# Self-attention of a hybrid decoder layer: value products per head with the values stationary in two f32r parts, and the output weights split inside the stage

## Chip, cores and metric

The kernel runs on one core of one Trainium2 chip. The time is device time in microseconds of one execution of the whole layer. Engines are called by the letters of the profile: PE (matmul), DVE (VectorE), ACT (ScalarE), POOL (GpSimd), SP (the engine that issues most DMAs).

## What is computed

One layer with three sub-layers over 1024 positions of width 1024, in f32. Only the first, the hybrid token mixer, is touched. Its part C is causal attention with 8 heads, query and key width 96, value width 64:

```
sc = einsum('bqhd,bkhd->bhqk', q_blk, k) * scale
mask = key_pos <= q_pos
p = softmax(where(mask, sc, -inf))
o = einsum('bhqk,bkhd->bqhd', p, v)
...
return concatenate([ret, sgu, mla], axis=-1) @ w_out
```

The 512 columns of `mla` are the last four of the eight 128-row slices over which the product with `w_out` (1024x1024) sums.

## The kernel before

The layer is a sequence of stages with a barrier between two of them: `project`, `prepare`, `attend`, `mix_out`, `cross_attend`, `experts`, `overflow`. Inside a stage each engine runs a list written out by hand and waits on counting semaphores. Two stages matter here.

**`attend`.** The work is cut into 48 units. For the first four query tiles (128 queries each, i = 0 to 3) a unit is a pair of heads, for i = 4 to 7 it is one head. The outer loop goes over i, the inner one over heads. For each unit PE makes the scores (queries stationary, up to 512 keys moving, f32, L704), DVE adds the causal mask to the diagonal 128 columns (L784) and takes the negated row maximum (L788, L790), ACT takes the exponential with the row sum (L748, L751), PE transposes the probabilities 128 columns at a time (L714), DVE copies the first and ACT the second transposed bank to SBUF (L797, L760), and PE multiplies (L725): the transposed probabilities are stationary, and 64 columns of values move, in f32. At the end of a query tile DVE divides by the row sums (L773, L774) and leaves `mix_mla` with the tokens in the partitions. Scores, transposes and outputs have two PSUM buffers each. In each round PE issues scores of unit u, values of unit u-2, transposes of unit u-1. Meanwhile SP loads `w_out` and fills DRAM buffers with zeros (L685 to L690).

**`mix_out`.** For each of 8 token tiles PE transposes eight 128x128 blocks of the mixer's output (L866), ACT rounds them to a high f32r part (L906), DVE makes the low part by subtraction (L924), and PE sums 8 slices x 2 halves x 3 products of high and low parts (L883 to L885). The weights are split in the same way, eight slices of 1024 columns, on ACT (L902) and DVE (L935), after the first tile's parts. DVE then waits for `x` and two broadcast gains (`loaded`) before it makes the parts of the second tile. SP loads the weights of the next stage after the last split.

In the functions below, `P` is 128, `MH` 8, `MV` 64, `NT` 8, `KD` 8, `S` and `D` 1024. `k.x` are tiles shared by the stages. In SBUF, `at(name, kb, shape)` places a tile at an offset in KB.

Of the kernel before, what the change touches and what calls it, by code (L numbers as in the profile page):

```python
# [15 lines left out]
P = 128  # L16
# [76 lines left out]
def over(ap, shape):  # L93
    return ap.broadcast_to(shape)
# [562 lines left out]
def attend(nc, k):  # L657
    at, A, cst = k.at, k.dram, k.cst
    prob = at("prob", 12, [P, 2, 2, 4 * P])
    probT = at("prob_T", 20, [P, 2, 2, 4 * P])  # L660
    nmx = at("neg_max", 28, [P, 2, 2])
    rsum = at("row_sum", 28.0625, [P, NT, MH])
    rinv = at("row_inv", 28.5, [P, NT, MH])
    zeros = at("zeros", 185, [P, ROW])
    ident = cst[:, C_ID:C_ID + P]
    units = [(i, h) for i in range(NT) for h in range(0, MH, 2 if i < 4 else 1)]

    scored = k.sem("scored")
    max_ready = k.sem("max_ready")
    exps = k.sem("exps")  # L670
    p_t = k.sem("p_t")
    pT_copied = k.sem("pT_copied")
    pT_copied_act = k.sem("pT_copied_act")
    pv_done = k.sem("pv_done")
    o_taken = k.sem("o_taken")
    dve_chain, zeroed = k.sem("chain3"), k.sem("zeroed")
    with nc.psum_tensor("s_ps", [P, 2, 2, 512], f32) as sps, \
# [4 lines left out]
        @block.sync  # L682
        def _(sp):
            for s in range(KD):
                sp.dma_start(k.w_out_raw[:, s, :], A["w_out"][s * P:(s + 1) * P, :]).then_inc(k.w_out_loaded, 16)  # L685

            sp.wait_ge(zeroed, 1)
            for t in range(SLOTS // P):
                sp.dma_start(k.xs_dram[t * P:(t + 1) * P, :], zeros[:]).then_inc(k.rows_zeroed, 16)
                sp.dma_start(k.z_dram[t * P:(t + 1) * P, :], zeros[:, 0:D]).then_inc(k.rows_zeroed, 16)  # L690

        def parts(u):

            i, h = units[u]
            return [(h, 0, i + 1), (h + 1, 0, i + 1)] if i < 4 else [(h, 0, 4), (h, 4, i + 1)]

        @block.tensor
        def _(pe):
            def scores(u):
                i = units[u][0]  # L700
                if u >= 2:
                    pe.wait_ge(exps, 2 * (u - 1))
                for j, (h, a, z) in enumerate(parts(u)):
                    last = pe.matmul(sps[:, u % 2, j, 0:(z - a) * P], k.qT[0:MQ, h, i * P:(i + 1) * P], k.kT[0:MQ, h, a * P:z * P],  # L704
                                     start=True, stop=True)
                last.then_inc(scored, 1)

            def turn(u):
                pe.wait_ge(exps, 2 * (u + 1))
                for j, (h, a, z) in enumerate(parts(u)):  # L710
                    if u:
                        pe.wait_ge(pT_copied if j == 0 else pT_copied_act, u)
                    for m in range(z - a):
                        last = pe.transpose(tps[:, j, m * P:(m + 1) * P], prob[:, u % 2, j, m * P:(m + 1) * P], ident)  # L714
                    last.then_inc(p_t, 1)

            def values(u):
                i, h0 = units[u]
                pe.wait_ge(pT_copied, u + 1)
                pe.wait_ge(pT_copied_act, u + 1)  # L720
                if h0 == 0 and i >= 2:
                    pe.wait_ge(o_taken, i - 1)
                for j, (h, a, z) in enumerate(parts(u)):
                    for m in range(a, z):
                        last = pe.matmul(ops[:, i % 2, h * MV:(h + 1) * MV], probT[:, u % 2, j, (m - a) * P:(m - a + 1) * P],  # L725
                                         k.v[:, m, h * MV:(h + 1) * MV], start=(m == 0), stop=(m == i))
                last.then_inc(pv_done, 1)

            n = len(units)
            for u in range(n + 2):  # L730
                if u < n:
                    scores(u)
                if 0 <= u - 2:
                    values(u - 2)
                if 0 <= u - 1 < n:
                    turn(u - 1)

        @block.scalar
        def _(act):
            for u in range(len(units) + 1):  # L740
                if u < len(units):
                    i, h = units[u]
                    act.wait_ge(max_ready, u + 1)
                    if u >= 2:
                        act.wait_ge(p_t, 2 * (u - 1))
                    if i < 4:
                        for j in range(2):
                            act.activation(prob[:, u % 2, j, 0:(i + 1) * P], sps[:, u % 2, j, 0:(i + 1) * P], ACT.Exp,  # L748
                                           bias=nmx[:, u % 2, j:j + 1], accum_out=rsum[:, i, h + j:h + j + 1]).then_inc(exps, 1)
                    else:  # L750
                        act.activation(prob[:, u % 2].rearrange("p j n -> p (j n)")[:, 0:(i + 1) * P],  # L751
                                       sps[:, u % 2].rearrange("p j n -> p (j n)")[:, 0:(i + 1) * P], ACT.Exp,
                                       bias=nmx[:, u % 2, 0:1], accum_out=rsum[:, i, h:h + 1]).then_inc(exps, 2)
                if u >= 1:
                    v = u - 1
                    _, a, z = parts(v)[1]
                    act.wait_ge(p_t, 2 * (v + 1))
                    if v >= 2:
                        act.wait_ge(pv_done, v - 1)
                    act.activation(probT[:, v % 2, 1, 0:(z - a) * P], tps[:, 1, 0:(z - a) * P], ACT.Copy).then_inc(pT_copied_act, 1)  # L760

        @block.vector
        def _(dve):
            chain = [0]

            def link(ins):
                chain[0] += 1
                ins.then_inc(dve_chain, 1)
                dve.wait_ge(dve_chain, chain[0])

            def take(i):
                dve.wait_ge(pv_done, units.index((i + 1, 0)) if i + 1 < NT else len(units))
                link(dve.reciprocal(rinv[:, i, :], rsum[:, i, :]))  # L773
                dve.tensor_tensor(k.mixB[:, i, :].rearrange("p (h d) -> p h d", d=MV),  # L774
                                  ops[:, i % 2, :].rearrange("p (h d) -> p h d", d=MV),
                                  over(rinv[:, i, :, None], [P, MH, MV]), ALU.mult).then_inc(o_taken, 1)

            for u in range(len(units) + 1):
                if u < len(units):
                    i, h = units[u]  # L780
                    dve.wait_ge(scored, u + 1)
                    s = sps[:, u % 2].rearrange("p j n -> p (j n)")
                    d = sps[:, u % 2, :, i * P:(i + 1) * P] if i < 4 else s[:, None, i * P:(i + 1) * P]
                    link(dve.tensor_tensor(d, d, over(cst[:, None, C_MASK:C_MASK + P], [P, d.shape[1], P]), ALU.add))  # L784
                    if u >= 2:
                        dve.wait_ge(exps, 2 * (u - 1))
                    if i < 4:
                        dve.tensor_reduce(nmx[:, u % 2, :], sps[:, u % 2, :, 0:(i + 1) * P], AX.X, ALU.max, negate=True).then_inc(max_ready, 1)  # L788
                    else:
                        dve.tensor_reduce(nmx[:, u % 2, 0:1], s[:, 0:(i + 1) * P], AX.X, ALU.max, negate=True).then_inc(max_ready, 1)  # L790
                if u >= 1:
                    v = u - 1
                    _, a, z = parts(v)[0]
                    dve.wait_ge(p_t, 2 * v + 1)
                    if v >= 2:
                        dve.wait_ge(pv_done, v - 1)
                    dve.tensor_copy(probT[:, v % 2, 0, 0:(z - a) * P], tps[:, 0, 0:(z - a) * P]).then_inc(pT_copied, 1)  # L797
                    if units[v][0] and v == units.index((units[v][0], 0)) + 1:
                        take(units[v][0] - 1)
            take(NT - 1)  # L800

        @block.gpsimd
        def _(pool):
            pool.memset(zeros[:], 0.0).then_inc(zeroed, 1)


# [5 lines left out]
def mix_out(nc, k):  # L812
# [3 lines left out]
    wraw = k.w_out_raw  # L816
    whi = at("wo_hi", 105, [P, KD, D], f32r)
    wlo = at("wo_lo", 137, [P, KD, D], f32r)
# [20 lines left out]
    with nc.psum_tensor("mixT_ps", [P, 2, 2, 512], f32) as tps, \  # L839
# [4 lines left out]
        def _(sp):  # L844
# [5 lines left out]
            sp.wait_ge(w_lo, KD)  # L850
# [5 lines left out]
            sp.wait_ge(mix_t, NT)  # L856
# [3 lines left out]
        def _(pe):  # L860
            def turn(t):
                if t >= 2:
                    pe.wait_ge(m_lo, t - 1)
                for j in range(KD):
                    src = k.mixA if j < 4 else k.mixB
# [5 lines left out]
            for t in range(NT):  # L871
# [1153 lines left out]
```

## Time and profile before

| | |
|---|---|
| median of 3 runs | 1056.36 us (1054.65 to 1058.7) |
| profiled execution | 1056.7 us, its span 1054.4 us |
| PE busy | 976.8 us, 93% |
| DVE busy | 607.2 us, 58% |
| ACT busy | 353.9 us, 34% |
| POOL busy | 191.0 us, 18% |
| mean granted PE clock | 0.962 |

A busy PE is not a PE at its peak: matmuls overlap in the pipeline and the profile models their ends. How long a stream of them takes is read from the starts. An f32 matmul appears as two records, an f32r matmul and a transpose as one. In the trace both types are written f32, except where DVE or ACT writes fp32r.

### The profile page before, as it was taken

To read this page: it belongs to the slowest core of one execution; us is meant where nothing else is said; L and a number is where in the kernel's file an instruction comes from. 1 tells how busy PE (TensorE), PEld (TensorE's weight loads), DVE (VectorE), ACT (ScalarE), POOL (GpSimd) and SP (SyncE) were. 2 spreads that over 40 slices of the span, in tenths; PEclk is the share of its full clock that TensorE was granted. 3 is DMA by queue.
4 is the path that set the end of the run, shared out by engine and by line. 5 is a ranking of instruction groups with operands and counts; after the bars stand their busy time and mean duration, and the time that the engine had idled before them with its cause. 6 is when DMAs were issued, how large, how long until landed. Compare 5 with 4: busy or idle time off the path is not lost. (4 is left out here: it accounts for less than half of the span.)

```text
span 1054.4 us, 15610 instructions
## 1 busy us (share of the span) xinstructions
PE 976.8 (93%) x5507; PEld 820.1 (78%) x5507; DVE 607.2 (58%) x1268; ACT 353.9 (34%) x736; POOL 191.0 (18%) x272
## 2 busy tenths in 40 slices
PE   7999999999899999899999999997289999999995
PEld 5898877767778887688885888886279898888984
DVE  6634341777566655455472455347526767676675
ACT  6112121343444333410013232331134445444442
POOL 0022100121000000012220000002414453434334
PEclk9999999999699999899999999998579999999998
DMA  9022010000798000370203200031748889899972
GB/s 334 13 77 80 1 61 1 1 1 1 305 413 328 1 1 2 120 277 3 80 1 123 80 1 1 1 133 69 300 153 261 296 269 316 280 319 314 318 286 89
DMA packets 63735, 150.46 MB, mean 143 GB/s; under 512 B 10304, under 2 KB 12608, under 8 KB 63680
## 3 DMA queue, kind: packets, MB, share of 16 engines
q1 hardware_dynamic: 54720, 132.77, 35.8%
q0 software_dynamic: 8960, 16.96, 4.3%
q8 instruction: 34, 0.56, 0.2%
q14 instruction: 21, 0.17, 0.1%
HBM read 109.46 MB, written 54.92 MB: 156 GB/s over the span
## 5 line engine op out<-in xcount | busy, mean ns | idle before, releaser
L1627 PEld LDWEIGHTS h_ps<-xgT,e_gate_up 128*128 128x128 f32 x1024 | 156.3, 192 | 4.2 <-issue 1.9
L1627 PE MATMUL h_ps<-xgT,e_gate_up 128*128 128x176 f32 x1024 | 157.8, 316 | 1.7 <-ACT xgT L1661 1.7
L245 PE MATMUL unit_ps<-whi,xhi 128*128 128x512 f32 (+1 forms) x256 | 98.3, 384 | 9.6 <-DVE wlo L276 9.6
L246 PE MATMUL unit_ps<-wlo,xhi 128*128 128x512 f32 (+1 forms) x256 | 97.8, 382 | 0.0
L247 PE MATMUL unit_ps<-whi,xlo 128*128 128x512 f32 (+1 forms) x256 | 97.7, 382 | 0.0
L725 PEld LDWEIGHTS o_ps<-mla_v,prob_T 128*128 128x128 f32 x576 | 72.6, 197 | 15.4 <-issue 10.5
L704 PE MATMUL s_ps<-mla_kT,mla_qT 96*128 96x512 f32 (+3 forms) x192 | 74.3, 515 | 3.4 <-PEq L1978 3.4
L725 PE MATMUL o_ps<-mla_v,prob_T 128*128 128x64 f32 x576 | 72.3, 276 | 2.8 <-ACT prob_T L760 2.5
L245 PEld LDWEIGHTS unit_ps<-whi,xhi 128*128 128x128 f32 x256 | 48.6, 190 | 18.1 <-DVE xlo L315 7.3
L247 PEld LDWEIGHTS unit_ps<-whi,xlo 128*128 128x128 f32 x256 | 48.5, 189 | 7.8
L246 PEld LDWEIGHTS unit_ps<-wlo,xhi 128*128 128x128 f32 x256 | 48.6, 190 | 7.5
L1692 ACT ACTIVATE ln_junk<-z,z_neg_mean 128x1024 f32<-128x1024 f32 (+1 forms) x32 | 36.8, 1149 | 52.1 <-DVE z_neg_mean L1751 51.6
L1746 DVE SCALAR_TENSOR_TENSOR z<-y_ps,slot_weight,x_rows 128x512 f32<-128x512 f32 (+1 forms) x64 | 45.7, 746 | 14.0 <-PE y_ps L1639 13.8
L751 ACT ACTIVATE prob<-s_ps,neg_max 128x640 f32<-128x640 f32 (+3 forms) x32 | 30.6, 955 | 67.7 <-issue 63.9
L883 PE MATMUL mix_acc<-wo_hi,mixT_hi 128*128 128x512 f32 x128 | 51.1, 399 | 2.2 <-DVE wo_lo L935 2.2
L1637 PE MATMUL y_ps<-e_dn_hi,h_hi 128*128 128x512 f32 (+1 forms) x128 | 52.0, 406 | 0.9 <-DVE z L1746 0.9
L704 PEld LDWEIGHTS s_ps<-mla_kT,mla_qT 96*128 96x128 f32 x192 | 35.2, 211 | 22.6 <-issue 20.9
L884 PE MATMUL mix_acc<-wo_lo,mixT_hi 128*128 128x512 f32 x128 | 50.5, 395 | 0.0
L885 PE MATMUL mix_acc<-wo_hi,mixT_lo 128*128 128x512 f32 x128 | 50.4, 394 | 0.0
L1639 PE MATMUL y_ps<-e_dn_hi,h_lo 128*128 128x512 f32 (+1 forms) x128 | 50.2, 393 | 0.0
L1638 PE MATMUL y_ps<-e_dn_lo,h_hi 128*128 128x512 f32 (+1 forms) x128 | 50.0, 391 | 0.0
L1714 DVE SCALAR_TENSOR_TENSOR ln_out<-ln_tmp,z_rstd,ln_b 128x1024 f32<-128x1024 f32 (+1 forms) x34 | 42.0, 1277 | 5.1 <-POOL z_rstd L1594 5.1
(280 smaller groups left out, 1930.9 us busy)
## 6 DMA issues: line engine op xcount, KB each, us to landing
e_gate_up<-w_gu SPq DMA_DIRECT2D x16, 2048.0 KB, 11.1
e_down_raw<-w_dn SPq DMA_DIRECT2D x16, 1024.0 KB, 5.4
slot_rows<-zeros SPq DMA_DIRECT2D x22, 522.0 KB, 14.8
slot_sums<-zeros SPq DMA_DIRECT2D x22, 512.0 KB, 15.2
x_rows<-slot_rows SPq DMA_DIRECT2D x16, 522.0 KB, 4.7
slot_sums<-z SPq DMA_DIRECT2D x16, 512.0 KB, 4.5
wraw<-w_in SPq DMA_DIRECT2D x24, 256.0 KB, 4.6
xraw<-xT SPq DMA_DIRECT2D x8, 512.0 KB, 6.8
```

The lines of the kernel that those rows point to most:

```text
L245: pe.matmul(o, hi, whi[:, s, 0:w], start=(s == 0), stop=False)
L246: pe.matmul(o, hi, wlo[:, s, 0:w], start=False, stop=False)
L247: last = pe.matmul(o, lo, whi[:, s, 0:w], start=False, stop=(s == KD - 1))
L704: last = pe.matmul(sps[:, u % 2, j, 0:(z - a) * P], k.qT[0:MQ, h, i * P:(i + 1) * P], k.kT[0:MQ, h, a * P:z * P], start=True, stop=True)
L725: last = pe.matmul(ops[:, i % 2, h * MV:(h + 1) * MV], probT[:, u % 2, j, (m - a) * P:(m - a + 1) * P], k.v[:, m, h * MV:(h + 1) * MV], st ...
L883: pe.matmul(o, hi, whi[:, s, c], start=(s == 0), stop=False)
L884: pe.matmul(o, hi, wlo[:, s, c], start=False, stop=False)
L885: last = pe.matmul(o, lo, whi[:, s, c], start=False, stop=(s == KD - 1))
L1627: end = pe.matmul(hps[:, m, gu * CAP:(gu + 1) * CAP], gate_up[:, b, s, w], xT[:, s, :], start=(s == 0), stop=(s == KD - 1))
L1637: pe.matmul(out, hi, dn_hi[:, b, w, :], start=(f == 0), stop=False)
L1638: pe.matmul(out, hi, dn_lo[:, b, w, :], start=False, stop=False)
L1639: return pe.matmul(out, lo, dn_hi[:, b, w, :], start=False, stop=(f == 1))
```

## The change

- The units are now 64, one head and one query tile each: the outer loop goes over heads, the inner over query tiles from the largest (i = 7, 1024 keys) down to i = 0.
- Each transposed bank is read twice: ACT copies it as a high f32r part, then DVE subtracts that part from the bank to make the low part. Both are kept for four query tiles (a group, g = 1 for i = 4 to 7, g = 0 for i = 3 to 0).
- Three steps after a group's last unit (`LATER`), PE multiplies: the values of 128 keys are stationary, high part in 64 columns and low part in the other 64, and up to 512 queries move, once with the high and once with the low probabilities. ACT moves one half of the result across partitions (`low_over`), DVE adds (`add`).
- For each pair of heads and group, DVE inverts row sums, POOL spreads them over 64 columns, PE transposes them (4 transposes), ACT copies them out, POOL multiplies. The result is already transposed, so `mix_out` transposes four blocks a tile and not eight.
- Six of the eight slices of `w_out` are split inside `attend`, one in each of the heads 2 to 7; two are left in `mix_out`. The loads of `w_out` and the zero fills are spread over the heads, and `mix_out` issues the loads of the next stage without waiting.
- The mask is an addition on DVE before and after.

```diff
-    units = [(i, h) for i in range(NT) for h in range(0, MH, 2 if i < 4 else 1)]
+    units = [(h, i) for h in range(MH) for i in reversed(range(NT))]
+    n = len(units)
+    def jobs(u):
+        i = units[u][1]
+        return [(0, i + 1)] if i < G else [(0, G), (G, i + 1)]
+    turned_by = [sum(len(jobs(v)) for v in range(u + 1)) for u in range(n)]
+    groups = [(h, g) for h in range(MH) for g in (1, 0)]
+    group_end = [NT * h + (G - 1 if g else NT - 1) for h, g in groups]
+    LATER = 3
+    SPLIT_AT = {NT * (s + 2) + 6: s for s in range(6)}
+    V_AT = {NT * (h - 1) + 4: h for h in range(2, MH)}
...
         @block.tensor
+            def next_bank():
+                q = at_bank[0]
+                at_bank[0] += 1
+                if q >= 2:
+                    kind, index = bank_order[q - 2]
+                    if kind == "probs":
+                        pe.wait_ge(lo_done, index + 1)
+                    else:
+                        pe.wait_ge(inv_copied, index + 1)
+                return q % 2
...
+            def values(kk):
+                h, g = groups[kk]
+                pe.wait_ge(lo_done, turned_by[group_end[kk]])
+                pe.wait_ge(v_lo, h + 1)
+                if kk >= 2:
+                    pe.wait_ge(o_added, kk - 1)
+                tiles = G * g + G
+                for m in range(tiles):
+                    c = slice(max(0, m - G * g) * P, 512)
+                    v = v_parts[:, h % 2, m, :]
+                    pe.matmul(ops[:, kk % 2, c], v, pT_hi[g][:, m, c], start=(m == 0), stop=False)
+                    last = pe.matmul(ops[:, kk % 2, c], v, pT_lo[g][:, m, c], start=False, stop=(m == tiles - 1))
+                last.then_inc(pv_done, 1)
...
+            for s in range(n + LATER + 1):
+                if s < n:
+                    scores(s)
+                kk = group_at(s)
+                if kk is not None:
+                    values(kk)
+                if 1 <= s <= n:
+                    turn(s - 1)
+                if kk is not None and groups[kk][0] % 2:
+                    turn_inverses(kk)
 
         @block.scalar
...
+            for s in range(n + LATER + 1):
+                kk = group_at(s)
+                if kk is not None and s < n:
+                    exp(s)
+                if 1 <= s <= n:
+                    high(s - 1)
+                if kk is None and s < n:
+                    exp(s)
+                if kk is not None:
+                    low_over(kk)
+                    if groups[kk][0] % 2:
+                        take_inverses(kk)
+                if s in V_AT:
+                    split_v(V_AT[s])
+                if s in SPLIT_AT:
+                    w = SPLIT_AT[s]
+                    act.wait_ge(k.w_out_loaded[w], 16)
+                    act.activation(whi[:, w, :], wraw[:, w, :], ACT.Copy).then_inc(w_hi, 1)
 
         @block.vector
...
+            for s in range(n + LATER + 2):
+                if s < n:
+                    largest(s)
+                if s - 2 in group_end and groups[group_end.index(s - 2)][0] % 2:
+                    invert(group_end.index(s - 2))
+                if 1 <= s <= n:
+                    low(s - 1)
+                if group_at(s - 1) is not None:
+                    add(group_at(s - 1))
+                if s in SPLIT_AT:
+                    w = SPLIT_AT[s]
+                    dve.wait_ge(w_hi, w + 1)
+                    dve.tensor_tensor(wlo[:, w, :], wraw[:, w, :], whi[:, w, :].bitcast(f32), ALU.subtract).then_inc(w_lo, 1)
...
 def mix_out(nc, k):
...
-                for j in range(KD):
-                    src = k.mixA if j < 4 else k.mixB
-                    last = pe.transpose(tps[:, t % 2, j // 4, (j % 4) * P:(j % 4 + 1) * P],
-                                        src[:, t, (j % 4) * P:(j % 4 + 1) * P], ident)
+                for j in range(4):
+                    last = pe.transpose(tps[:, t % 2, 0, j * P:(j + 1) * P], k.mixA[:, t, j * P:(j + 1) * P], ident)
...
-                    if t == 0:
-                        pe.wait_ge(w_lo, s + 1)
+                    if t == 0 and s >= 6:
+                        pe.wait_ge(w_lo, s - 5)
...
-            for s in range(KD):
-                dve.wait_ge(w_hi, s + 1)
+            for s in range(6, KD):
+                dve.wait_ge(w_hi, s - 5)
                 dve.tensor_tensor(wlo[:, s, :], wraw[:, s, :], whi[:, s, :].bitcast(f32), ALU.subtract).then_inc(w_lo, 1)
```

`largest` is mask and maximum, `low` the subtraction for each bank of a unit, `high` the copy for each bank. `exp(u)` waits for `max_ready` of u; `scores(u)` for the exponential of u-2.

## Rows read from the trace of the kernel before

**Rows 1.** Windows: span, PE, PEld, DVE, ACT, POOL busy, granted clock, DMA share, GB/s.

```profile
265.00:268.00 3.00, 0.00 (x0) 0.00 (x0) 2.04 (x7) 1.36 (x3) 0.16 (x1) 0.97 0.00 0
...
268.20:276.00 7.80, 6.69 (x29) 6.17 (x30) 3.97 (x10) 2.96 (x15) 0.97 (x1) 0.50 0.86 325
276.00:290.00 14.00, 13.79 (x65) 11.51 (x63) 7.11 (x16) 5.88 (x25) 0.00 (x0) 0.68 1.02 393
290.00:303.00 13.00, 12.41 (x76) 9.22 (x76) 8.23 (x14) 6.35 (x20) 0.00 (x0) 1.00 1.03 415
...
398.00:438.90 40.90, 37.97 (x257) 30.29 (x255) 20.11 (x29) 14.03 (x25) 0.00 (x0) 0.99 0.01 1
...
444.40:457.30 12.90, 12.82 (x50) 10.41 (x51) 9.12 (x9) 6.03 (x7) 0.00 (x0) 0.87 1.00 370
457.30:539.00 81.70, 81.70 (x386) 68.19 (x385) 40.88 (x47) 6.23 (x7) 17.12 (x14) 1.00 0.22 77
```

**Rows 2.** Timeline of one unit at i = 7: start, duration, engine, line, operation.

```profile
400.88 1.88 PE L704 MATMUL s_ps<-mla_kT,mla_qT 96*128 96x512 f32 x4
...
402.60 1.67 PE L725 MATMUL o_ps<-mla_v,prob_T 128*128 128x64 f32 x14
...
402.80 0.30 DVE L784 TENSOR_TENSOR s_ps<-s_ps,constants 128x128 f32<-128x128 f32 x1 [1.36 <-PE s_ps L704]
403.13 1.23 DVE L790 TENSOR_REDUCE neg_max<-s_ps 128x1 f32<-128x1024 f32 x1
...
404.11 1.04 PE L714 MATMUL t_ps<-constants,prob 128*128 128x128 f32 x8
404.44 1.11 ACT L751 ACTIVATE prob<-s_ps,neg_max 128x1024 f32<-128x1024 f32 x1 [2.42 <-issue]
404.75 0.69 DVE L797 COPY prob_T<-t_ps 128x512 f32<-128x512 f32 x1 [0.39 <-PE t_ps L714]
...
404.99 1.88 PE L704 MATMUL s_ps<-mla_kT,mla_qT 96*128 96x512 f32 x4
...
405.46 0.19 ACT L751 ACTIVATION_READ_ACCUMULATOR prob<-s_ps,neg_max 128x1 f32 x1
405.55 0.58 ACT L760 ACTIVATE prob_T<-t_ps 128x512 f32<-128x512 f32 x1
```

**Rows 3.** Groups by form: busy us, mean ns of one, idle before.

```profile
L725 PE MATMUL o_ps<-mla_v,prob_T 128*128 128x64 f32 x576 | 72.3, 276 | 2.8 <-ACT prob_T L760 2.5
L883 PE MATMUL mix_acc<-wo_hi,mixT_hi 128*128 128x512 f32 x128 | 51.1, 399 | 2.2 <-DVE wo_lo L935 2.2
...
L924 DVE TENSOR_TENSOR mixT_lo<-mixT_ps,mixT_hi 128x1024 fp32r<-128x1024 f32 x8 | 9.7, 1218 | 5.2 <-ACT mixT_hi L906 3.4 <-DMA ln_b<-ln_mix_b 1.7
...
L751 ACT ACTIVATE prob<-s_ps,neg_max 128x896 f32<-128x896 f32 x8 | 8.1, 1008 | 18.0 <-issue 18.0
...
L790 DVE TENSOR_REDUCE neg_max<-s_ps 128x1 f32<-128x640 f32 x8 | 6.6, 825 | 0.3
...
L642 POOL TENSOR_TENSOR ret_kd<-qk,constants 128x256 f32<-128x256 f32 x8 | 5.8, 727 | 0.1
```

**Rows 4.** Timeline of the start of the output projection, from 441.5 us.

```profile
441.53 0.78 PE L866 MATMUL mixT_ps<-constants,mix_mla 128*128 128x128 f32 x4
441.84 7.68 ACT L902 ACTIVATE wo_hi<-w_out_raw 128x1024 fp32r<-128x1024 f32 x8
...
443.12 9.16 DVE L935 TENSOR_TENSOR wo_lo<-w_out_raw,wo_hi 128x1024 fp32r<-128x1024 f32 x8
...
444.48 0.47 PE L883 MATMUL mix_acc<-wo_hi,mixT_hi 128*128 128x512 f32 x1 [2.17 <-DVE wo_lo L935]
...
445.61 0.63 PE L884 MATMUL mix_acc<-wo_lo,mixT_hi 128*128 128x512 f32 x1
...
453.97 1.23 DVE L924 TENSOR_TENSOR mixT_lo<-mixT_ps,mixT_hi 128x1024 fp32r<-128x1024 f32 x1 [1.69 <-DMA ln_b<-ln_mix_b]
...
457.89 0.48 PE L883 MATMUL mix_acc<-wo_hi,mixT_hi 128*128 128x512 f32 x1
```

More of the change, by code:

```diff
@@ new lines, in attend, with group_at @@
+    n = len(units)
[6 more added lines that the diff above has]
+    LATER = 3
+    def group_at(s):
+        return group_end.index(s - LATER) if s - LATER in group_end else None
+    bank_order = []
+    for s in range(1, n + LATER + 1):
+        if s <= n:
+            bank_order += [("probs", turned_by[s - 1] - len(jobs(s - 1)) + j) for j in range(len(jobs(s - 1)))]
+        if group_at(s) is not None and groups[group_at(s)][0] % 2:
+            bank_order.append(("inverses", group_at(s) // 4 * 2 + group_at(s) % 2))
@@ L708, in turn @@
             def turn(u):
[L709 to L714, printed above, removed]
-                    last.then_inc(p_t, 1)
[L717 to L726, printed above, removed]
-                last.then_inc(pv_done, 1)
@@ L729, in _ @@
[L729 to L736, printed above, removed]
+                pe.wait_ge(exps, u + 1)
+                for a, z in jobs(u):
+                    b = next_bank()
+                    for m in range(a, z):
+                        last = pe.transpose(tps[:, b, (m - a) * P:(m - a + 1) * P], prob[:, u % 2, m * P:(m + 1) * P], ident)
+                    last.then_inc(p_t, 1)
@@ new lines, in turn_inverses @@
+            def turn_inverses(kk):
+                h, g = groups[kk]
+                pe.wait_ge(spread_out, inverse_index(kk) + 1)
+                b = next_bank()
+                for j in range(G):
+                    last = pe.transpose(tps[:, b, j * P:(j + 1) * P], spread[:, j].rearrange("p h d -> p (h d)"), ident)
+                last.then_inc(inv_t, 1)
+            for s in range(n + LATER + 1):
[8 more added lines that the diff above has]
+                    turn_inverses(kk)
@@ L738, in _ @@
         @block.scalar
         def _(act):
[L740 to L760, printed above, removed]
@@ new lines, in high @@
+            def high(u):
+                h, i = units[u]
+                g, c = i // G, (i % G) * P
+                first = turned_by[u] - len(jobs(u))
+                if h and i % G == G - 1:
+                    act.wait_ge(pv_done, 2 * h - 1 - g)
+                for j, (a, z) in enumerate(jobs(u)):
+                    act.wait_ge(p_t, first + j + 1)
+                    act.activation(pT_hi[g][:, a:z, c:c + P], tps[:, bank_order.index(("probs", first + j)) % 2, 0:(z - a) * P].rearrange("p (m q) -> p m q", q=P),
+                                   ACT.Copy).then_inc(hi_done, 1)
@@ new lines, in low_over, with take_inverses @@
+            def low_over(kk):
+                h, g = groups[kk]
+                act.wait_ge(pv_done, kk + 1)
+                if kk >= 2:
+                    act.wait_ge(o_added, kk - 1)
+                to, fro = (slice(0, MV), slice(MV, P)) if h % 2 == 0 else (slice(MV, P), slice(0, MV))
+                act.activation(low_half[to, kk % 2, :], ops[fro, kk % 2, :], ACT.Copy).then_inc(low_copied, 1)
+            def take_inverses(kk):
+                r = inverse_index(kk)
+                act.wait_ge(inv_t, r + 1)
+                if r:
+                    act.wait_ge(mixed, r)
+                act.activation(r_all[:], tps[:, bank_order.index(("inverses", r)) % 2, :], ACT.Copy).then_inc(inv_copied, 1)
@@ L778, in _ @@
[L778 to L799, printed above, removed]
@@ L800, in _, with largest @@
-            take(NT - 1)
+            def largest(u):
+                i = units[u][1]
+                dve.wait_ge(scored, u + 1)
+                d = sps[:, u % 2, i // G, (i % G) * P:(i % G + 1) * P]
+                dve.tensor_tensor(d, d, cst[:, C_MASK:C_MASK + P], ALU.add).then_inc(masked, 1)
+                dve.wait_ge(masked, u + 1)
+                if u >= 2:
+                    dve.wait_ge(exps, u - 1)
+                dve.tensor_reduce(nmx[:, u % 2:u % 2 + 1], sps[:, u % 2].rearrange("p j n -> p (j n)")[:, 0:(i + 1) * P], AX.X, ALU.max, negate=True)\
+                   .then_inc(max_ready, 1)
@@ new lines, in low @@
+            def low(u):
+                i = units[u][1]
+                g, c = i // G, (i % G) * P
+                first = turned_by[u] - len(jobs(u))
+                for j, (a, z) in enumerate(jobs(u)):
+                    dve.wait_ge(hi_done, first + j + 1)
+                    dve.tensor_tensor(pT_lo[g][:, a:z, c:c + P], tps[:, bank_order.index(("probs", first + j)) % 2, 0:(z - a) * P].rearrange("p (m q) -> p m q", q=P),
+                                      pT_hi[g][:, a:z, c:c + P].bitcast(f32), ALU.subtract).then_inc(lo_done, 1)
@@ new lines, in invert, with add @@
+            def invert(kk):
+                h, g = groups[kk]
+                dve.wait_ge(exps, group_end[kk] + 1)
+                t = slice(G * g, G * g + G)
+                dve.reciprocal(rinv[:, t, h - 1:h + 1], rsum[:, t, h - 1:h + 1]).then_inc(inverted, 1)
+            def add(kk):
+                h, g = groups[kk]
+                dve.wait_ge(low_copied, kk + 1)
+                if kk >= 4:
+                    dve.wait_ge(mixed, inverse_index(kk) - 1)
+                r = slice(MV * (h % 2), MV * (h % 2) + MV)
+                dve.tensor_tensor(o_sum[r, kk % 2, :], ops[r, kk % 2, :], low_half[r, kk % 2, :], ALU.add).then_inc(o_added, 1)
@@ new lines, in scale @@
+            def scale(kk):
+                h, g = groups[kk]
+                pool.wait_ge(o_added, kk + 1)
+                pool.wait_ge(inv_copied, inverse_index(kk) + 1)
+                pool.tensor_tensor(k.mixBT[:, h // 2, 512 * g:512 * g + 512], o_sum[:, kk % 2, :], r_all[:], ALU.mult).then_inc(mixed, 1)
+            pool.memset(zeros[:], 0.0).then_inc(zeroed, 1)
+            split_v(0)
+            split_v(1)
+            for s in range(n + LATER + 2):
+                if s in V_AT:
+                    split_v(V_AT[s])
+                if s - 2 in group_end and groups[group_end.index(s - 2)][0] % 2:
+                    spread_inverses(group_end.index(s - 2))
+                if group_at(s - 1) is not None and groups[group_at(s - 1)][0] % 2:
+                    scale(group_at(s - 1))
@@ L899, in _ @@
                 if t == 1:
[L900 to L901 removed]
+                    for s in range(6, KD):
+                        act.wait_ge(k.w_out_loaded[s], 16)
                         act.activation(whi[:, s, :], wraw[:, s, :], ACT.Copy).then_inc(w_hi, 1)
@@ L932, in _ @@
             rest(0)
-            for s in range(KD):
-                dve.wait_ge(w_hi, s + 1)
+            for s in range(6, KD):
+                dve.wait_ge(w_hi, s - 5)
                 dve.tensor_tensor(wlo[:, s, :], wraw[:, s, :], whi[:, s, :].bitcast(f32), ALU.subtract).then_inc(w_lo, 1)
@@ L1940, in program @@
     k.v = at("mla_v", 169, [P, NT, MW])
-    k.w_out_raw, k.w_out_loaded = at("w_out_raw", 30, [P, KD, D]), k.sem("w_out_loaded")
+    k.wo_hi, k.wo_lo = at("wo_hi", 105, [P, KD, D], f32r), at("wo_lo", 137, [P, KD, D], f32r)
+    k.w_out_raw, k.w_out_loaded = at("w_out_raw", 137, [P, KD, D]), [k.sem(f"w_out_loaded{s}") for s in range(KD)]
     k.wuq = at("w_uq", 192, [P, QR // P, MH * MQ])
```

125 lines of the change are left out of this document (74 added, 51 removed).

## The prediction

> **What bounds the kernel now.** The page gives PE 93% of the span, but only two stages are touched, so I read the windows of those [rows 1]. The attention stage runs from 268.3 to 438.9 us, 170.6 us. From 290 us on PE is hardly ever idle, while DVE is busy for about half the time and ACT for a third. The timeline of one unit [rows 2] says why: scores take 1.72 us (400.88 to 402.60), value products 1.51 us (402.60 to 404.11), transposes 0.88 us (404.11 to 404.99), and the next scores start at once. That is 4.11 us, all PE. So today every wait on DVE or ACT is hidden. In the output projection PE is busy throughout from 457.3 us [rows 1], but its first tile waits for the weights' parts and its second for parts made late [rows 4].
>
> **PE's share of the change.** Value products now are 576 records of 64 columns, some 0.1 us apart [rows 2, 3]: 7 us for a head. After, an f32r product of 512 columns costs 0.227 us: 81.7 us less 48 transposes of 0.11, over 336 products [rows 1]. A head's upper group has 16 products (10 of 512 columns, two each of 384, 256 and 128), 3.1 us; the lower has 8, 1.25 us. Under 384 columns f32r has no row: bounds are nothing, and the 512 price; I take it in proportion, not below 0.11. The six affected products of a head can add at most 0.6 us. Four transposed inverses for each group of a pair add 0.45 us a head. PE's sum for a head is then scores 7.7 (0.214 us for each 128 keys [rows 2]), transposes 4.1, values 4.3, inverses 0.45: 16.6 us, or 133 us for eight. Before it was about 150. On PE alone some 17 us are won.
>
> **DVE's share.** One step costs a mask 0.34 (402.80 to 403.13), a maximum of 0.29 to 1.23 us, and now a subtraction over every transposed bank, not a copy of half of them. Both slopes are 0.133 us for 128 columns: (1.23 - 0.825)/3 [rows 2, 3], and 1.218 for 1024 [rows 3]. With about 0.08 us of overlap between successive instructions, a 512-column subtraction takes 0.61. A head costs masks 2.7, maxima 5.4, subtractions 5.8, two additions 1.2, six eighths of a weight slice of 1.15 (9.16/8 [rows 4]) 0.9: 16.0 us. ACT's head: exponentials 5.8 (1.10 for 1024, 0.11 less for each 128 [rows 2, 3]), copies 4.7, moves, value split, weights 3.2: 13.7. So PE, DVE and ACT would each need 14 to 17 us a head, with only two buffers between them. The order of each list decides.
>
> **A walk through one head.** Zero is when exp(7) has finished. From [rows 2]: transposes start 0.15 us after an exponential; four are readable 0.64 after their start (404.11 to 404.75), each fewer takes 0.11 off; scores are readable 0.20 after their last slot; maximum to exponential 0.08; a subtraction frees a bank for PE after 0.12; an exponential's sum is read 0.09 after its busy time. Step by step for an even head without a weight slice:
>
> exp(6): turn(7) 0.15 to 1.05, high(7) until 1.88, exp(6) done 2.9. exp(5): low(7) ends DVE's work at 2.64, then mask and maximum of 5 until 3.94, exp(5) done 5.0. Now the group step. PE puts the lower group's values (2.34 to 3.6) before turn(6), and ACT does exp(5) before high(6), so high(6) starts at 4.9 and ends at 5.9. low(6) follows until 6.7 and holds both banks: turn(5) cannot start before 6.35. DVE then runs without a break: maximum(4), low(5), add, maximum(3), and exp(4) ends at 8.8, exp(3) at 11.1, exp(2) at 13.1. At 12.2 PE, after the scores of 1, starts the upper group's values, until 15.3, and turn(2) stands behind them. DVE and ACT wait for it, DVE 2.5 us. exp(1) is done at 14.6. Then high(2) to 16.3, low(2) to 16.9, maximum(0), exp(0) at 18.0, low(1), add, maximum(7) of the next head (its scores readable at 18.0, DVE free at 18.3), exp(7) at 21.2. **A head takes 21.2 us, not 16.6.**
>
> With a weight slice (heads 2 to 7), ACT's copy (0.96) stands after the move of the half result, until 17.8, and DVE waits for it in order; its subtraction ends at 19.0, and maximum(0), low(1), add and maximum(7) stand behind. Next exp(7) at 23.3: +2.1, of which DVE waits 1. For odd heads turned inverses add 0.5 to 0.9 at the upper group. At the lower group, in the following head, the third bank use must wait for low(6) at 6.35, and scores(4) stand behind it on PE: +1.5. V splits stand in ACT's gaps. POOL's operations are on other buffers a step or more ahead; 512 elements have no row, bounds 0.7 and 2.9 us (727 ns for 256 [rows 3], once to four times); I take 1.45. Only the last multiplication shows.
>
> **Sum for the stage.** Start: scores(7) at half clock, as PE sits idle before the stage and the clock is 0.50 after [rows 1]: 3.4 + 0.2 + 1.6 + 0.1 + 1.2 = 6.5 us. Heads 0 to 6: 20.9 (no lower group yet, but slow clock), 22.0, 24.8, 23.8, 24.8, 23.8, 24.8, together 164.9. Head 7: exp(0) at 20.6, then turn, high, low 1.1, values 1.5, move, inverses 1.1, add 0.6, POOL 1.45: 26.1. Total 197.5, +27 against 170.6. PE would be busy for about 70% of it.
>
> **The clock.** Between heads with a slice PE has scores(7) done at 17.8, idles until 20.3, works 1.6 us and idles 1.6. In the rows a gap of this kind, 442.3 to 444.5, is followed by products 0.43 us apart (445.61, mean 0.63 long, against 0.39) and a mean clock of 0.87 over 12.9 us, so 3.4 us at half rate [rows 1, 4]; that is 1.2 GHz for 2.4. If it falls, turn(7) and scores(5) are late: about 2 us a head. Against it: 290 to 303 us stayed at 1.00 with small gaps [rows 1]. Bounds 0 and 6 x 2 = 12; I take 3. The Trainium skill (TensorE: Matmul & The Clock Gate, "A second HAM failure mode: psum-queue depth-cycling") says that PE idling briefly between groups while it cycles PSUM buffers makes the clock oscillate; by it the full 12 would be paid.
>
> **The projection.** Its first product no longer waits for a split slice: four transposes instead of eight, two short copies and two subtractions, about 3.1 us after the start and not 5.6. But DVE makes the second tile's parts only after `x` and the gains have landed, at 453.97, 15.1 us in [rows 4]. Plus 1.3 for two subtractions: the second tile starts at 16.5, today at 19.0 (457.89): -2.4. If the next stage's loads, issued at once behind, slow that landing (the DMAs are full there, 1.00 [rows 1]), nothing is won. Then six tiles have four transposes less, 6 x 0.45 = 2.7. The later start of `wq`'s load is hidden by two tiles, some 20 us. Together -5, bounds -6 and -2. Six weight splits leave this stage, where the transfers already hid most of them, and go to the path of the other. Zero fills end about 20 us before attention does; used a stage later.
>
> Sum: +27 +3 -5 = +25 on the profiled execution's 1056.7 (span 1054.4); the median is 0.3 lower: 1081 us.
>
> **Rivals.**
> (a) The walk holds, 1065 to 1095: 0.58.
> (b) The clock falls at every change of head and in the small steps too, at 3 to 4 us a head, or small steps have waits that I missed: 1095 to 1110. For: gaps of 442 to 444. Chance 0.12.
> (c) The other side: PE stays the bound. Engines run ahead through the two buffers, so that a head takes PE's 16.6 plus about 1. The price is 8 x 17.6 + 12 for both ends = 153, -18, and -5 of the projection: 1034. It decides below 20.5 us a head: (170.6 + 5 - 6.5 - 26.1)/7 = 20.4. For: PE was the bound before with the same two buffers [rows 2]. Against: ACT and DVE are in order, and DVE alone needs 16. Chance 0.18 for anything faster.
> (d) In between, a head of 20.5 to 22 us, the small waits shorter than I walked: 1052 to 1065. Chance 0.12, a third of it within the bound.
>
> Likeliest case's own range: 1065 to 1095. Eight in ten: 1052 to 1098. A run of this kernel tells 0.5%, 5 us, from no change. Slower 0.76, within 0.05, faster 0.19.
>
> **What would show it.** The same stage windows: attention 190 to 205 us, PE busy near 70%, DVE the fullest of the four. DVE maxima at i = 7 some 21 to 25 us apart, 2 us more from head 2 on. L-lines of the new value products 0.227 apart for 512 columns, in bursts of 3.1 us, with DVE and ACT idle behind each. DVE waiting for ACT's weight copy about 1 us six times. First product of the projection about 3 us after its start. The prediction is wrong if the exponentials of i = 7 lie less than 20.5 us apart, if PE is still above 90%, or if products under 384 columns cost several times their share.

## The result

The changed kernel takes 1093.5 us (median of 4, 1089.7 to 1095.8), the kernel before 1057.5. The ratio is 1.034, with a 95% interval from 1.030 to 1.038: slower by 36 us. The forecast was 1081 us, in a range of 1052 to 1098.

The page of the changed kernel: busy time of the engines, and the slices of PE and its clock.

```profile
span 1093.2 us, 15043 instructions
...
PE 971.5 (89%) x5123; PEld 792.2 (72%) x5123; DVE 632.8 (58%) x1364; ACT 398.9 (36%) x824; POOL 218.2 (20%) x296
...
PE   7999999998877777869999999998459999999995
...
PEclk9999999999998888879999999998669999999998
```

PE shows gaps in slices 11 to 18, which hold the attention stage, and from slice 13 on, 328 us, the clock is below 0.9 in each of them. The windows of the stage, of two stretches in it and of the projection (columns as in [rows 1]):

```profile
268.20:479.40 211.20, 162.84 (x704) 109.38 (x705) 130.57 (x254) 117.71 (x262) 25.89 (x26) 0.88 0.36 131
276.00:290.00 14.00, 11.60 (x63) 8.15 (x62) 9.53 (x19) 8.74 (x21) 0.00 (x0) 1.00 0.10 39
...
340.00:346.00 6.00, 5.35 (x15) 3.12 (x16) 4.32 (x8) 2.89 (x7) 0.00 (x0) 0.59 1.02 419
...
479.40:575.10 95.70, 94.10 (x418) 77.60 (x419) 46.08 (x58) 10.72 (x19) 17.75 (x15) 0.96 0.36 132
```

Attention takes 211.1 us (from 268.3) where it took 170.6, +40.5. The projection takes 95.7 where it took 100.0, -4.3. The stages behind, untouched, are 2.6 us longer in this execution. Together that is the 38.8 us between the spans of the two profiled executions. PE is busy for 163 us of the 211 (77%), DVE for 131, ACT for 118: nobody is full.

DVE's row maxima of the largest query tile mark the heads (timeline, DVE):

```profile
273.04 1.22 DVE L869 TENSOR_REDUCE neg_max<-s_ps 128x1 f32<-128x1024 f32 x1
...
292.88 1.23 DVE L869 TENSOR_REDUCE neg_max<-s_ps 128x1 f32<-128x1024 f32 x1
...
314.60 1.23 DVE L869 TENSOR_REDUCE neg_max<-s_ps 128x1 f32<-128x1024 f32 x1
...
340.74 1.23 DVE L869 TENSOR_REDUCE neg_max<-s_ps 128x1 f32<-128x1024 f32 x1
...
366.60 1.23 DVE L869 TENSOR_REDUCE neg_max<-s_ps 128x1 f32<-128x1024 f32 x1
```

I number the heads 0 to 7 and measure each from its own such maximum to that of the next head. Heads 0 to 3 take 19.8, 21.7, 26.1 and 25.9 us, heads 4 to 6 then 27.0, 26.2 and 28.1. Head 2 is the first with a weight slice. Its end, in the order of time:

```profile
331.95 0.59 PE L773 MATMUL o_ps<-prob_T_hi,v_parts 128*128 128x512 f32 x1
...
335.07 0.27 PE L774 MATMUL o_ps<-prob_T_lo,v_parts 128*128 128x128 f32 x1
...
335.18 0.51 PE L760 MATMUL t_ps<-constants,prob 128*128 128x128 f32 x3
...
335.97 1.88 PE L751 MATMUL s_ps<-mla_kT,mla_qT 96*128 96x512 f32 x4
...
336.24 0.60 ACT L829 ACTIVATE o_low_half<-o_ps 64x512 f32<-64x512 f32 x1
336.25 0.56 DVE L878 TENSOR_TENSOR prob_T_lo<-t_ps,prob_T_hi 128x384 fp32r<-128x384 f32 x1 [2.29 <-ACT prob_T_hi L820]
...
336.74 1.04 ACT L857 ACTIVATE wo_hi<-w_out_raw 128x1024 fp32r<-128x1024 f32 x1
...
337.81 1.23 DVE L907 TENSOR_TENSOR wo_lo<-w_out_raw,wo_hi 128x1024 fp32r<-128x1024 f32 x1 [1.01 <-ACT wo_hi L857]
...
339.28 0.29 DVE L869 TENSOR_REDUCE neg_max<-s_ps 128x1 f32<-128x128 f32 x1
...
340.12 0.33 PE L760 MATMUL t_ps<-constants,prob 128*128 128x128 f32 x1 [2.27 <-ACT prob L809]
...
343.25 1.97 PE L760 MATMUL t_ps<-constants,prob 128*128 128x128 f32 x8 [0.53 <-ACT prob L809]
```

The burst of value products ends at 335.1, and only then are three blocks transposed for which DVE had waited 2.29 us. Then DVE waits 1.01 us for ACT's weight copy, and the small maximum of 339.28 comes behind the subtraction. PE stands still for 2.27 us until 340.12. Its next eight transposes, at 343.25, take 1.97 us and not 1.04: half clock, a mean of 0.59 over 340 to 346.

### The profile page after: what moved, and what is told of

It is laid out like the page before. It is cut to its first block and busy times, and to the rows that moved or that the text cites. A ratio compares the mean times of both kernels' runs of the same rounds, so it can differ in the third digit from the quotient of the medians.

```text
span 1093.2 us, 15043 instructions
## 1 busy us (share of the span) xinstructions
PE 971.5 (89%) x5123; PEld 792.2 (72%) x5123; DVE 632.8 (58%) x1364; ACT 398.9 (36%) x824; POOL 218.2 (20%) x296
## 5 line engine op out<-in xcount | busy, mean ns | idle before, releaser
L751 PE MATMUL s_ps<-mla_kT,mla_qT 96*128 96x512 f32 (+1 forms) x192 | 84.8, 558 | 3.4 <-PEq L2110 3.4
L760 PE MATMUL t_ps<-constants,prob 128*128 128x128 f32 x288 | 50.1, 307 | 39.6 <-ACT prob L809 30.2
L760 PEld LDWEIGHTS t_ps<-constants,prob 128*128 128x128 f32 x288 | 35.7, 155 | 64.7 <-ACT prob L809 58.7
L878 DVE TENSOR_TENSOR prob_T_lo<-t_ps,prob_T_hi 128x512 fp32r<-128x512 f32 (+1 forms) x96 | 50.8, 553 | 47.0 <-ACT prob_T_hi L820 46.4
L809 ACT ACTIVATE prob<-s_ps,neg_max 128x1024 f32<-128x1024 f32 (+3 forms) x64 | 47.4, 741 | 42.9 <-DVE neg_max L869 42.6
L820 ACT ACTIVATE prob_T_hi<-t_ps 128x512 fp32r<-128x512 f32 (+1 forms) x96 | 44.1, 489 | 42.5 <-PE t_ps L760 42.3
L1877 DVE SCALAR_TENSOR_TENSOR z<-y_ps,slot_weight,x_rows 128x512 f32<-128x512 f32 (+1 forms) x64 | 45.7, 745 | 16.5 <-PE y_ps L1770 12.3
```

The source lines that it names most:

```text
L760: last = pe.transpose(tps[:, b, (m - a) * P:(m - a + 1) * P], prob[:, u % 2, m * P:(m + 1) * P], ident)
L878: dve.tensor_tensor(pT_lo[g][:, a:z, c:c + P], tps[:, bank_order.index(("probs", first + j)) % 2, 0:(z - a) * P].rearrange("p (m q) -> p m ...
```

## Experiments

All start from the changed kernel. They change places and owners of work, one adds work that nobody uses, and one leaves work out. "Less" is against the changed kernel's median of 1093.5 us; each ratio is to the kernel before, which measured 1056.4 to 1057.8 beside these runs.

**The low part of the weight slices on POOL.**

```diff
-  dve.tensor_tensor(wlo[:, w, :], wraw[:, w, :], whi[:, w, :].bitcast(f32), ALU.subtract)
+  pool.tensor_tensor(wlo[:, w, :], wraw[:, w, :], whi[:, w, :].bitcast(f32), ALU.subtract)
```

> The low part of each weight slice inside the attention stage is made by POOL, not by DVE; all else is as in the changed kernel (1093.5 us). Theory (serial chain between the engines' ordered lists, and the clock that falls in the gap it leaves): each of heads 2 to 7 loses the subtraction (1.15 us) and DVE's wait for ACT's copy (1.0 to 1.6) from the chain, 6 x 2.3 = 14 us, and PE's gap before the last transposes of a head shrinks from 2.3 us to under 1, so that the clock stays up there: another 10 us. Time 1066 to 1074, maxima of i = 7 about 22 us apart in all heads. Rival A (the clock falls at changes of head anyway): 14 us alone, 1079. Rival B (the slices lie beside PE's bursts and are hidden, the time comes from the work of the low parts of the probabilities): under 4 us, 1090 or more.

Measured 1077.0 us, ratio to the kernel before 1.0195 (1.0168 to 1.0221), 16.5 less than the changed kernel. Attention ends 15.5 us earlier, at 463.9. Heads 2 to 6 take 23.5, 22.5, 25.1, 22.5 and 26.6 us. The slices are on the path, against rival B. The clock stays at 1.00 in heads 2, 3 and 5 and still falls in heads 4 and 6 (0.93, 0.87): the result lies between the theory and rival A.

**Products that only keep PE busy.**

```diff
+  fill = {0: 2, 7: 1}.get(units[u][1], 0)
...
+  pe.matmul(tps[:, b, :], ident, cst[:, C_DEC:C_DEC + 512], start=True, stop=True)
   pe.wait_ge(exps, u + 1)
```

> Extra f32 products of 512 columns on constants, two before the transposes of i = 0 and one before those of i = 7 in every head, into the bank that these transposes then overwrite. They stand where PE waits for the exponential, and their results are not used. Theory (the granted clock falls after PE's gap and costs 2 us a head): the clock stays at 1.00 from head 2 on and the time falls by 10 to 14 us, to 1080 to 1084, although PE has 21 us more to do. Rival A (the low clock is hidden behind DVE's chain): no change, 1093. Rival B (the products are not all inside the gaps and delay the transposes): slower, 1095 to 1105.

Measured 1084.4 us, ratio 1.0269 (1.0243 to 1.0294), 9 less (7 by the ratios), with more work on PE. Its stage, and PE after the same head's end as above:

```profile
268.20:472.40 204.20, 169.93 (x753) 110.27 (x754) 129.69 (x254) 116.72 (x262) 25.96 (x26) 0.96 0.37 135
```

```profile
340.09 1.88 PE L761 MATMUL t_ps<-constants 128*128 128x512 f32 x4
342.52 0.33 PE L766 MATMUL t_ps<-constants,prob 128*128 128x128 f32 x1 [0.55 <-ACT prob L815]
...
345.65 1.09 PE L766 MATMUL t_ps<-constants,prob 128*128 128x128 f32 x8 [0.44 <-ACT prob L815]
```

The eight transposes now take 1.09 us, and the stage's mean clock is 0.96, not 0.88. It still fell three times after the start, in heads 2, 5 and 6. Heads 3 and 4 were at full clock from end to end. Their windows, first in the changed kernel, then here:

```profile
340.74:366.60 25.86, 20.95 (x90) 13.86 (x89) 16.66 (x33) 14.94 (x34) 2.13 (x3) 0.87 0.41 152
366.60:393.61 27.01, 20.16 (x89) 13.85 (x88) 16.66 (x32) 15.10 (x33) 4.13 (x4) 0.87 0.30 107
```

```profile
343.13:367.02 23.89, 20.49 (x96) 13.29 (x95) 16.38 (x33) 14.83 (x34) 2.13 (x3) 1.00 0.44 165
367.02:391.81 24.79, 19.85 (x95) 12.87 (x94) 16.46 (x32) 14.88 (x33) 4.14 (x4) 1.00 0.34 120
```

They are 2.0 and 2.2 us shorter, and 23.9 and 24.8 us is what the walk gave for them without a fall of the clock (23.8 and 24.8). The fillers themselves are not free: heads 1 and 2, whose clock is hardly another, are 0.8 us longer than in the changed kernel. So the low clock is on the path, at 2 us a head or more. The expected 10 to 14 us were nearly reached.

**Value products in four parts behind the transposes.**

```diff
-  LATER = 3
+  LATER = 5
...
+  for m in range(q * tiles // 4, (q + 1) * tiles // 4):
...
+  for v, end in enumerate(group_end):
+      if 2 <= s - end <= 5:
+          values(v, s - end - 2)
```

> A group's value products are cut into four parts, issued behind the transposes of the steps 2 to 5 after the group's last unit, and not in one burst before the transposes of step 3; the move of the half result, the sum and the inverses come 5 steps after the group and not 3. Theory (the burst of 3.1 us stands in front of transposes for which ACT and DVE wait 2.1 to 2.5 us, and the lower group's burst shifts a step): 1.5 to 2.5 us less for each of 8 heads, 12 to 18 us, 1076 to 1082. Rival (DVE's own work is the bound, a stall that goes there comes back elsewhere): under 5 us, 1089 or more.

Measured 1070.5 us, ratio 1.0135 (1.0107 to 1.0163), 23 less, beyond the theory's 12 to 18. Heads 0 and 1, which have no slice, gain only 0.5 and 0.6 us. Heads 3 and 5 take 21.1 us at full clock, as head 1 does (21.1): with the burst moved, their slice costs nothing and their clock does not fall. That is where the theory counted too little. DVE's waits for ACT's copies before a subtraction (L878 in the changed kernel, L881 here) fall from 46.4 to 28.8 us:

```profile
L878 DVE TENSOR_TENSOR prob_T_lo<-t_ps,prob_T_hi 128x512 fp32r<-128x512 f32 (+1 forms) x96 | 50.8, 553 | 47.0 <-ACT prob_T_hi L820 46.4
```

```profile
L881 DVE TENSOR_TENSOR prob_T_lo<-t_ps,prob_T_hi 128x512 fp32r<-128x512 f32 (+1 forms) x96 | 50.6, 552 | 29.6 <-ACT prob_T_hi L823 28.8
```

The first row is the changed kernel, the second this one. The granted clock of the whole run rises as well, 0.948 to 0.963.

**The mask on PE.**

```diff
+  last = pe.matmul(sps[:, u % 2, i // G, (i % G) * P:(i % G + 1) * P], ident, cst[:, C_MASK:C_MASK + P], start=False, stop=True)
   last.then_inc(scored, 1)
...
-  dve.tensor_tensor(d, d, cst[:, C_MASK:C_MASK + P], ALU.add).then_inc(masked, 1)
```

> The causal mask is added by PE, as one more f32 product of 128 columns (identity times mask) into the scores' bank, not by DVE. DVE has 64 x 0.34 = 21 us less, PE 64 x 0.23 = 15 us more. Theory (DVE's ordered list is on the path in most steps, PE is not the bound): 8 to 16 us less, 1078 to 1086. Rival (PE is still the bound as before the change): 10 to 15 us more, 1103 to 1108.

Measured 1075.8 us, ratio 1.0181 (1.0143 to 1.0219), 18 less, beyond the theory's 8 to 16. PE is not the bound: it has 64 more products to do, some 15 us by my estimate, and the kernel gets faster. But the 18 us are not the price of the masks. Head 0 takes 19.9 us and head 1 21.4, against 19.8 and 21.7: where the clock was full before, 2.7 us of masks a head were worth 0.0 and 0.3. The gain is in heads 2 to 6, where the clock is now 1.00 throughout. Heads 3 and 4:

```profile
338.03:361.03 23.00, 19.74 (x106) 14.46 (x105) 14.30 (x25) 14.85 (x34) 1.84 (x2) 1.00 0.46 170
361.03:385.02 23.99, 19.07 (x105) 14.26 (x104) 14.53 (x24) 14.70 (x33) 4.42 (x4) 1.00 0.34 123
```

Against the same heads at full clock with fillers (23.9 and 24.8) that is 0.9 and 0.8 less, against the changed kernel 2.9 and 3.0. The gap before PE's last transposes of head 3 is 1.09 us and not 1.66. Most of what this run gains is the clock.

**Without the low parts of the probabilities.**

```diff
-  pe.matmul(ops[:, kk % 2, c], v, pT_hi[g][:, m, c], start=(m == 0), stop=False)
-  last = pe.matmul(ops[:, kk % 2, c], v, pT_lo[g][:, m, c], start=False, stop=(m == tiles - 1))
+  last = pe.matmul(ops[:, kk % 2, c], v, pT_hi[g][:, m, c], start=(m == 0), stop=(m == tiles - 1))
...
-  low(s - 1)
```

> Leaves work out: the low parts of the probabilities are not made and not multiplied, so each transposed bank is read once, by ACT, and PE's burst is half as long; the weight slices, masks and the rest are as in the changed kernel (1093.5 us). It prices the second read of the banks. Theory (DVE's subtractions, 5.8 us a head, stand on the path in nearly every step, and the burst's second half, 1.5 us, in one): 5 to 7 us less a head, 40 to 56 us, 1038 to 1053, below the kernel before. Rival (the waits between engines set the time, not the amount of work): under 25 us, 1070 or more.

One execution, 1071.2 us: 22 less, where I expected 40 to 56; the run's rival said under 25. Its stage and two of its groups:

```profile
268.20:455.09 186.89, 143.41 (x608) 92.33 (x609) 85.72 (x158) 116.42 (x262) 25.91 (x26) 0.88 0.40 148
```

```profile
L864 DVE TENSOR_TENSOR s_ps<-s_ps,constants 128x128 f32<-128x128 f32 x64 | 19.0, 298 | 71.8 <-PE s_ps L751 71.5
...
L904 DVE TENSOR_TENSOR wo_lo<-w_out_raw,wo_hi 128x1024 fp32r<-128x1024 f32 x6 | 7.4, 1225 | 21.9 <-ACT wo_hi L856 21.9
```

DVE has 45 us less to do and the stage is 24 us shorter. The rest has turned into waits for PE's scores (71.5 us, 18.3 before) and for ACT's weight copy (21.9, 7.9 before), at the same mean clock. My theory of this run, 5 to 7 us a head, falls: head 0, at full clock before and after, is 1.9 us shorter (18.0 against 19.8), and head 3 only 0.9, at a lower clock (0.79 against 0.87). The amount of DVE's work is not what sets the time. The run does not price the subtractions alone, as half of PE's value products are gone with them.

**All weight slices split in the projection.**

```diff
-  SPLIT_AT = {NT * (s + 2) + 6: s for s in range(6)}
+  SPLIT_AT = {}
```

(and the loops over slices in `mix_out` from 0, as before the change)

> Undoes one part: all eight slices of the output weights are split in the projection, as before the change, none inside attention. Theory: attention loses what POOL's version lost and ACT's copies too, 16 to 20 us; the projection's first product waits again for a slice and its first tile for the splits, 2 to 3 us more. Time 1075 to 1080. Rival (a split inside the stage is worth its place): the projection gives back 10 us or more, 1087 or above.

Measured 1066.0 us, ratio 1.0102 (1.0066 to 1.0137), 27 less, more than expected. Attention lasts 186.0 us, 25 less than 211.1, and the projection 96.9, 1.2 more than 95.7. That is not more than noise: the eight other versions that have the changed kernel's projection took 95.7 to 96.9. POOL's version, where ACT's copies stay in attention, is 9.7 us behind in that stage. Where both are at full clock (heads 3 and 5) the copy costs 0.8 us a head; the rest is mostly its clock, which falls in heads 4 and 6 and here stays full in heads 3 to 6.

**Three of them together, without and with the slices in attention.**

> POOL makes the weights' low parts, PE adds the mask, and the value products come in four parts behind the transposes: e1, e3 and e4 in one. Each alone gave 17, 23 and 18 us. Theory (one chain, from which each takes its own piece, until PE's sum of 16.6 + 1.8 us a head is near): maxima of i = 7 19 to 20 us apart, attention 163 to 172 us and not 211, time 1046 to 1054, level with the kernel before or just below. Rival (the three take the same gaps away, the clock's fall above all): about 30 us together, 1063.

> As the last one, but the weights are all split in the projection. Theory: with POOL's subtraction off the path the place of the split is worth only ACT's copy (1 us in six heads) against 2 to 3 us in the projection: within 4 us of the last one, 1044 to 1056. Rival (ACT's copies and POOL's subtraction still delay attention): 6 us or more faster than the last one.

The first moves the weights' low parts to POOL and the mask to PE and cuts the value products in four; the second also splits all weights in the projection. Measured 1060.9 us (1.0042, 1.0020 to 1.0063) and 1061.8 us (1.0033, 1.0000 to 1.0065). The three gave 57 us one by one and give 33 together, so the rival of the first was nearer: they share gaps and the clock's fall. The second is within 4 us of the first, as expected, though neither comes near the times I gave (1044 to 1056); with the chain shorter the place of the split hardly matters. In the first, the odd heads take 20.1 us, but heads 2, 4 and 6, each behind an odd one, 22.5 to 23.9.

**Two orders.** The first is ACT's:

```diff
-  if kk is not None and s < n:
-      exp(s)
   if 1 <= s <= n:
       high(s - 1)
-  if kk is None and s < n:
+  if s < n:
       exp(s)
```

> The version with POOL's weight parts, PE's mask and spread value products (1060.9 us), with one order changed on ACT: in the two group steps of a head the copy of the last unit's bank comes before the exponential, as in all other steps. Theory (the reversed order chains maximum, exponential, copy and subtraction in one step): up to 0.7 us a head at the lower group, 3 to 6 us less, 1055 to 1058. Rival (with the burst gone ACT is no longer late there): no change, 1059 to 1063.

The second is PE's, `turn_inverses` of a group after the next step's `scores`:

> The same version (1060.9 us), with PE's four transposes of inverses issued after the next unit's scores and not before them. In that version heads that follow an odd head are 2.4 to 3.8 us longer than the others, as PE waits there for a bank with the next scores behind it. Theory: that wait no longer holds the scores back, 1.5 to 3 us less in each of three heads, 4 to 9 us less, 1052 to 1057. Rival (ACT's copy of the inverses and its wait are the cost, wherever PE puts them): no change or 1 to 3 us more.

Measured 1054.6 us (0.9970, 0.9950 to 0.9990) and 1057.1 us (1.0005, 0.9984 to 1.0026). That is 6.3 us less than the first (3 to 6 expected) and 3.8 less (4 to 9 expected), so both theories hold near an edge of their range; the second gain is about as large as the noise of the two ratios. In each of the two, the heads after an odd one take 21.7 and 22.1 us and not 22.5 to 23.9. Part of that is again the clock: heads 4 and 6 had 0.93 before and have 1.00 now.

**Both, and a later wait in the projection** (`wait_ge(loaded, 160)` behind the second tile's parts):

> Both of these orders, and in the projection DVE waits for x and the gains after it has made the second tile's parts, not before. In the changed kernel the second tile's parts start only when the gains have landed, 15.4 us into the stage. Theory: the second tile's products follow the first's at once, 2 us less in the projection, with the two orders together 1045 to 1053, under the kernel before by 0.5 to 1%. Rival (the accumulation of x for the first tile waits for the same transfer and holds the third tile): the 2 us come back there, and the time is that of the orders alone, 1052 to 1057.

Measured 1053.3 us, ratio 0.9966 (0.9949 to 0.9983), the fastest of all and 3 to 4 us below the kernel before, within what I called no change. Its stage:

```profile
268.20:439.80 171.60, 157.94 (x832) 116.14 (x833) 107.55 (x184) 114.50 (x262) 40.03 (x32) 0.99 0.43 161
```

171.6 us against 170.6 before: attention is level, and what is won is in the projection (95.1 against 100.0). The later wait shows no gain of its own: 95.1 against 95.9 with ACT's order alone is within the 1.2 us by which equal projections differ. The first tile, which begins at half clock, is summed only at 455.9, 16 us into the stage, so the gains are there in time anyway.

## Why the prediction was right, and where it was off

**The mechanism** held: ordered lists, two buffers, and PE no longer the bound, which the fillers and the masks on PE show. A head without a slice was walked at 20.9 and 22.0 us and took 19.8 and 21.7. The named waits stand in the trace at their places: 2.3 us of DVE behind the burst (2.5 forecast), 1.0 or 1.6 for ACT's weight copy (1.0), PE's gap of 2.27 or 1.66 (2.5). The time is 12 us above the forecast, inside the range. Of the signs that I named, three came out otherwise: attention takes 211 us and not 190 to 205, PE is busy for 77% and not near 70%, and PE and not DVE is the fullest engine. Head 0, at 19.8 us, is under the 20.5 that I had named as a sign of being wrong; the mean of heads 0 to 6 is 25.0.

**The clock** is the term that was sized wrong. I took 3 of a possible 12 us. Heads 2 to 6 were walked at 24.8 or 23.8 and took 26.1, 25.9, 27.0, 26.2 and 28.1, 11 us more in sum, and their mean clock was 0.80 to 0.93. The last head and the tail were 26.1 and took about 29, at half clock for two stretches, one at the start and one around a gap of 3.37 us. The stage is 211.1, 11 above the forecast of 200.5, clock term included. That the clock is the reason is shown for heads 3 and 4: with fillers they keep it and come to the walked times within 0.1 us. That walk and time agree so closely is in part luck, as the fillers cost something too. The Trainium skill (TensorE: Matmul & The Clock Gate, "A second HAM failure mode: psum-queue depth-cycling") says that short idles of PE between groups of products make its clock go up and down. By it, the prediction said, the full 12 us would be paid; the trace agrees, with a fall in each of heads 2 to 6, and it was the better guide than my weight of a quarter.

**Rival (b)**, the clock's fall at every change of head, is thus half true: it falls in each head with a slice, but costs 2 us or a little more and not 3 to 4, and the small steps hold. The time is 1.5 us short of its band, so case (a) is right by its range with part of (b)'s mechanism in it.

**Small f32r products**: 0.17, 0.12 and 0.07 us apart for 384, 256 and 128 columns, at 1.0 clock. They are nearly in proportion down to 128, and the burst takes 3.2 us (3.1 forecast).

**DVE's list.** The sums of its work were right (131 us busy against 128). What I later expected of it, that the list is on the path in most steps, does not hold: at full clock the masks were worth 0.0 and 0.3 us of 2.7 in the heads without a slice and at most 0.9 with one, and the subtractions with half the value products 1.9 us in head 0.

**The weight slice** was priced at 2.1 us a head, with ACT's copy standing in part in a gap. Taking both away gave 25 us in six heads, 4.2 each, the clock included. At full clock the price was about right: heads 3 and 4 take 23.9 and 24.8 us with fillers and slices, 21.7 and 22.6 without slices, 2.2 us each, of which up to 0.9 can be the fillers.

**The inverses** at the lower group: PE waits 1.86 us for the bank (1.5 walked), and then the clock falls there too, to half from 323.8 to 327.5 us, which I had not seen.

**The projection**: first product 2.65 us after the start (3.1 forecast), second tile at 16.7 (16.5), in all -4.3 (-5), give or take the 1.2 us between equal projections. The next stage's loads did not delay `x` and the gains: they landed 15.4 us in, against 15.1 [rows 4].

**Rival (c)**, PE as the bound, needed 20.5 us a head. Over heads 0 to 6 only the last version comes there, with a mean of 20.4 us; the three parts together give 21.4.

What stays open: the clock's exact share of the 40 us. Five heads at 2 to 3 us each and the tail put it at some 10 to 18 us, an estimate from heads 3 and 4 (2.0 and 2.2 less with fillers, 2.9 and 3.0 with the mask on PE) and the tail's 3 us above the walk. The 2.6 us of the later stages need no cause: in the profiled executions of all versions, which run the same code there, these stages take 512.6 to 519.1 us.

## What to carry to other kernels

Cheaper work on the bound engine is worth nothing if its neighbours' ordered lists then close a loop around two buffers. Sum the engines first, and if they come within 20% of each other, walk one period: that gave each head within 6% where the clock stayed up. Do not price an instruction by its length, and read what its removal gave head by head, beside the granted clock: taking 21 us of masks off DVE gave 18, but 0.0 and 0.3 in the two heads where the clock had been full; taking away 51 us of subtractions with their products gave 22. And count the clock as part of each gap that a new wait opens on PE: here it cost about as much as the weight slice that opened the gap.

## What was not expected of the hardware

In the changed kernel the granted clock was at 0.5 (1.2 GHz) for 3 to 7 us, in part on busy work, once or twice in every head with a slice. PE had stood still shortly before: once for 2.27 us until 340.1, with the clock at half from 341.0, and once for 1.66 us until 365.7, with the clock at half from 368.3. A gap of 1.86 us, until 323.4, was also followed by such a fall; in the version that splits all slices in the projection, gaps of 1.85 us at the same place in heads 4 and 6 were not. POOL's subtraction of 1024 f32 columns took 2.35 us (DVE: 1.23) and that of 512 columns 1.28, and no engine waited for the first in attention.
